# Steps of the first attention moved between the slabs of the gates' projection, and modulation pieces placed anew

## What is computed

```python
u = rms_norm(h, norm_g[i])
z = u @ w_in[i]                       # queries, keys, latents and three gates g_a, g_b, g_c (2048 columns)
o_a = mla_mixer(...)                  # 6 heads
o_b = dsa_mixer(...)                  # 5 heads, each query sees its 64 best keys of an index score
o_c = diff_mixer(...)                 # 5 heads, the difference of two softmaxes, then a norm over the head
mixed = concat([o_a * silu(g_a), o_b * silu(g_b), o_c * silu(g_c)])
h = h + mixed @ w_o[i]
h = h + (p[i] @ w_ple[i]) * sigmoid(h @ w_pg[i])
```

## Time and profile before

| | |
|---|---|
| three runs | 3386.38, 3389.06 (median), 3389.70 us |
| profiled execution | 3384.65 us, span 3383.0 us |
| TensorE busy | 3164.3 us (94%) |
| VectorE busy | 2399.3 us (71%) |
| ScalarE busy | 1366.1 us (40%) |
| granted TensorE clock, mean | 0.957 of 2.4 GHz |
| HBM read | 700.26 MB, 208 GB/s |

### The profile page before, as it was taken

One profiled execution on the slowest core, in us unless ns is written; L12 is line 12 of the kernel. 1 busy time (PEld: TensorE's weight loads), 2 busy tenths in 40 slices (PEclk: granted clock), 3 DMA queues, 4 the chain that ended last, 5 costly groups with the idle time before them and its releaser, 6 DMA issues.

```text
span 3383.0 us, 58771 instructions
## 1 busy us (share of the span) xinstructions
PE 3164.3 (94%) x24402; PEld 2997.7 (89%) x24402; DVE 2399.3 (71%) x3266; ACT 1366.1 (40%) x1459; POOL 273.1 (8%) x530
## 2 busy tenths in 40 slices
PE   5999888989998889999999999999889999899998
PEld 5999658989997569999999999998679999799998
DVE  6876768987777678875777477666767977476464
ACT  4333344444334353444334334533654333434332
POOL 0000000000000000000010010000000232010000
PEclk9999869999999779999999999999999999899999
DMA  5776404766777018766677676476025765386553
GB/s 206 271 286 242 175 19 176 275 225 243 267 269 264 25 62 306 264 229 216 257 274 249 215 273 247 176 284 248 1 101 218 259 201 200 104 294 225 208 211 130
DMA packets 130932, 710.16 MB, mean 210 GB/s; under 512 B 16392, under 2 KB 16544, under 8 KB 71584
## 3 DMA queue, kind: packets, MB, share of 16 engines
q1 hardware_dynamic: 67392, 484.47, 40.1%
q0 software_dynamic: 61264, 214.93, 17.5%
q10 hardware_dynamic: 2064, 7.70, 0.6%
HBM read 700.26 MB, written 2.10 MB: 208 GB/s over the span
## 4 chain that ended last, share of the span: by engine, by line
PE 79%; DVE 10%; ACT 5%; issue 3%; DMA 3%; ACTq 0%; DVEq 0%; POOLq 0%
PE bank L510 23%; PE bank L506 21%; PE bank L507 21%; DMA aslab<-w_ada_dram 3%; ACT whi L1014 2%; DVE wlo L1523 2%; PE bank L603 2%; PE bank L835 1%; PE bank L814 1%; DVE aslab L1548 1%; DVE sc L1642 1%; PE bank L557 1%; PE bank L922 1%; PE bank L880 1%; ACT xs L1431 1%
## 5 line engine op out<-in xcount | busy, mean ns | idle before, releaser
L506 PE MATMUL bank<-uhi,whi 128*128 128x256 f32 x6720 | 1660.9, 287 | 70.7 <-issue 47.6
L507 PE MATMUL bank<-ulo,whi 128*128 128x256 f32 x6720 | 1649.1, 285 | 0.0
L1523 DVE TENSOR_TENSOR wlo<-raw,whi 128x2048 fp32r<-128x2048 f32 (+1 forms) x464 | 1053.4, 2272 | 686.6 <-ACT whi L1014 686.1
L1014 ACT CAST whi<-raw 128x2048 fp32r<-128x2048 f32 (+1 forms) x464 | 875.6, 1889 | 1596.1 <-PE bank L510 1537.5
L506 PEld LDWEIGHTS bank<-uhi,whi 128*128 128x128 f32 x6720 | 1303.6, 194 | 79.3 <-issue 69.6
L507 PEld LDWEIGHTS bank<-ulo,whi 128*128 128x128 f32 x6720 | 1303.6, 194 | 1.1
L510 PE MATMUL bank<-uhi,wlo 128*128 128x256 f32 x6720 | 882.6, 284 | 10.7 <-DVE wlo L1523 10.5
L510 PEld LDWEIGHTS bank<-uhi,wlo 128*128 128x128 f32 x6720 | 840.7, 192 | 12.7 <-DVE wlo L1523 12.7
L450 POOL DMA_DIRECT2D aslab<-w_ada_dram x384 | 202.8, 528 | 2855.0 <-DVE mod L1548 1542.0
L1548 DVE CUSTOM_DVE_ANT_0 aslab<-aslab,sil,cols 128x1024 f32<-128x1024 f32 x192 | 245.1, 1280 | 46.2 <-DMA aslab<-w_ada_dram 46.2
L1548 DVE CUSTOM_DVE_ANT_0 aslab<-aslab,sil,part 128x1024 f32<-128x1024 f32 x192 | 244.6, 1279 | 23.0 <-DMA aslab<-w_ada_dram 22.9
(11 more groups left out here) (265 smaller groups left out, 2493.6 us busy)
## 6 DMA issues: line engine op xcount, KB each, us to landing
aslab<-w_ada_dram POOLq DMA_DIRECT2D x384, 512.0 KB, 5.0
raw<-w_win_dram SPq DMA_DIRECT2D x96, 1024.0 KB, 4.8
raw<-w_wfi_dram SPq DMA_DIRECT2D x96, 1024.0 KB, 5.1
raw<-w_wfo_dram SPq DMA_DIRECT2D x48, 1024.0 KB, 4.8
raw<-w_wci_dram SPq DMA_DIRECT2D x48, 1024.0 KB, 4.9
raw<-w_wo_dram SPq DMA_DIRECT2D x32, 1024.0 KB, 4.9
raw<-w_wpg_dram SPq DMA_DIRECT2D x32, 1024.0 KB, 5.7
raw<-w_wqz_dram SPq DMA_DIRECT2D x32, 1024.0 KB, 4.8
```

The source lines that it names most:

```text
L506: nc.tensor.matmul(o, w_, xhi_, start=start, stop=False, skip_group_check=True)
L507: nc.tensor.matmul(o, w_, xlo_, start=False, stop=False, skip_group_check=True)
L1014: nc.scalar.copy(whi[:, s % 2, 0:n], raw[:, s, 0:n]).then_inc(s_hi, 1)
L1523: v.tensor_tensor(wlo[:, s, 0:n], raw[:, s, 0:n], whi[:, s % 2, 0:n].bitcast(F32), ALU.subtract).then_inc(s_lo, 1)
```

## The change

The input projection's gate columns, which were the first 4 of its 12 groups, become a run `ga` of their own behind `up`; `in` keeps 8 groups. The 24 steps of the first attention stand between the passes of the 16 slabs of `ga`: `UNIT_AT` gives 24 of the 32 points (a point lies between the high and the low pass of a slab, and one behind the slab) a step, from point 3 to point 30. Scores now use one PSUM bank and transposes one, since the slabs take four. ScalarE applies the gates' Silu as it drains each group of `ga` (before, in one instruction of 4096 columns in `up`). The sums and roots of the norm over heads c are split in three, their sums stand at points 28 and 30, and two quarters of `uhi`/`ulo` for run `o` are filled before the reciprocals. Some tiles move: the attention's operands leave `uhi`, which `ga` needs. Modulation pieces: `in` has 28 and 25 for 40 and 40, `v` 4 for 8, `fci` 28 for 40, `fxi` 42 for 40, `kvx` 4 for 0, `qz` 40 for 34, the second attention (`attn2`) 28 for 0, `ao` 19 for 17, `ci` 14 for 11, `co` 20 for 18. The total stays 384. The Silus of the condition vectors move with them.

```diff
-        run(f"in{l}", "T", "win", 12 * l, 12, ada=40)
-        run(f"v{l}", "N", "wv", 3 * l, 3, ada=8)
+        run(f"in{l}", "T", "win", 12 * l, 8, ada=(28, 25)[l])
+        run(f"v{l}", "N", "wv", 3 * l, 3, ada=4)
         run(f"up{l}", "S", "wup", l, 1, 6)
+        run(f"ga{l}", "T", "win", 12 * l + 8, 4)
...
-            run("kvx", "K", "wkv", 0, 1)
-            run("qz", "T", "wqz", 0, 8, ada=34)
-            run("ao", "T", "wao", 0, 4, ada=17)
-            run("ci", "T", "wci", 0, 12, ada=11)
-            run("co", "T", "wco", 0, 4, ada=18)
-        run(which + "i", "T", "wfi", 8 * j, 8, ada=32 if which == "f3" else 40)
+            run("kvx", "K", "wkv", 0, 1, ada=4)
+            run("qz", "T", "wqz", 0, 8, ada=40)
+            run("attn2", "A", None, 0, 0, ada=28)
+            run("ao", "T", "wao", 0, 4, ada=19)
+            run("ci", "T", "wci", 0, 12, ada=14)
+            run("co", "T", "wco", 0, 4, ada=20)
+        run(which + "i", "T", "wfi", 8 * j, 8, ada={"fc": 28, "fx": 42, "f3": 32}[which])
...
     def upto(p):
         if r["name"] == "in0":
-            return 32 * min(max(p - 4, 0), 31) // 31 + min(max(p - 39, 0), 8)
+            return min(max(p - 3, 0), 28)
         if r["name"] == "in1":
-            return r["ada"] * max(0, p - 4) // 44
+            return 16 * min(max(p - 3, 0), 13) // 13 + min(max(p - 22, 0), 9)
         if r["name"] == "ci":
             return min(p, r["ada"])
         if r["name"] in ("pg1", "fco", "fxo"):
             return r["ada"] * min(p, 13) // 13
-        if r["name"] in ("fci", "fxi"):
-            return min(p, 16) + 24 * max(0, p - 16) // 16
+        if r["name"] == "fci":
+            return min(p, 3) + 25 * max(0, p - 8) // 24
+        if r["name"] == "fxi":
+            return 18 * min(p, 16) // 16 + 24 * max(0, p - 16) // 16
+        if r["name"] == "f3i":
+            return min(p, 16) + max(0, p - 16)
+        if r["name"] == "attn2":
+            return r["ada"] * p // NP2
...
+UNIT_AT = {3 + 29 * t // (N1 + 3): t for t in range(N1 + 3)}
+TOP_AT = {13 * i // (TOPK // 8): i for i in range(TOPK // 8 + 1)}
...
+                def unit_step(t):
+                    if t < N1:
+                        u = N1 * l + t
+                        if t:
+                            pe.wait_ge(s_sd, u)
+                        scores(t, bank[5]).then_inc(s_s, 1)
+                    if 2 <= t < N1 + 2 and HAS_T1[t - 2]:
+                        i = t - 2
+                        tn = TN[N1 * l + i]
+                        pe.wait_ge(s_pr, N1 * l + i + 1)
+                        if tn > 1:
+                            pe.wait_ge(s_tc, tn - 1)
+                        for c in range(3):
+                            last = nc.tensor.transpose(bank[6][:, P * c:P * (c + 1)],
+                                                       scs[:, i % 3, P * c:P * (c + 1)], ident)
+                        last.then_inc(s_t, 1)
+                    if t >= 3 and HAS_T1[t - 3]:
+                        pe.wait_ge(s_tc, TN[N1 * l + t - 3])
+                        values(t - 3, pts[:, TN[N1 * l + t - 3] % 2, :]).then_inc(s_o, 1)
...
+                def point(n):
+                    t = UNIT_AT.get(n)
+                    if t is None:
+                        return
+                    unit_step(t)
+                    if t == N1:
+                        pe.wait_ge(s_osq, l + 1)
+                        pe.wait_ge(s_sd, N1 * (l + 1))
+                        subln_sum(0, bank[5])
+                    if t == N1 + 2:
+                        subln_sum(1, bank[6])
+                        pe.wait_ge(s_of, NT1 * (l + 1) - 1)
+                        subln_sum(2, bank[7])
+
                 pe.wait_ge(s_ir, 8 * l + 8)
-                softmax_units(N1 * l, N1, scores, transposes, values)
-
-                pe.wait_ge(s_osq, l + 1)
-                for c in range(3):
-                    n = 512 if c < 2 else 256
-                    last = nc.tensor.matmul(bank[5 + c][:, 0:n], ones[:, :], sq[:, 512 * c:512 * c + n],
-                                            start=True, stop=True)
-                last.then_inc(s_oss, 1)
+                r = RUN[f"ga{l}"]
+                for g in range(4):
+                    group(r, g, (r["e0"] + g) % 2, slab_t, None, lambda s, g=g: point(2 * (4 * g + s) + 1),
+                          lambda s, g=g: point(2 * (4 * g + s)))
...
+                def drain_ga(g):
+                    act.wait_ge(s_s, N1 * l + (6 if g else 4))
+                    summed(ga, g)
+                    for half in range(2):
+                        at = 1024 * g + 512 * half
+                        last = nc.scalar.activation(zz_t[:, at:at + 512],
+                                                    bank[2 * ((ga["e0"] + g) % 2) + half][:, :], ACT.Silu)
+                    last.then_inc(s_drain, 2)
+
+                ga, r = RUN[f"ga{l}"], RUN[f"ple{l}"]
+                for q in range(16):
+                    if q < 14:
+                        split(ga, (q + 2) // 4, (q + 2) % 4)
+                    else:
+                        split(r, 0, q - 14)
+                    if q == 14:
+                        act.wait_ge(s_p, 16 * (l + 1))
+                        nc.scalar.copy(uhi[:, 8:10, :], praw[:, :, :]).then_inc(s_uh, 4)
+                    if q % 4 == 3:
+                        drain_ga(q // 4)
+                    point(2 * q + 1)
+                    point(2 * q + 2)
+                act.wait_ge(s_aw, 2 * l + 2)
                 act.wait_ge(s_of, NT1 * (l + 1))
-                nc.scalar.activation(sq[:, 0:5 * T], zz_t[:, T * Z_CQ:T * (Z_CQ + 5)], ACT.Square)\
-                    .then_inc(s_osq, 1)
-
-                r = RUN[f"ple{l}"]
-                presplit(f"ple{l}")
-                act.wait_ge(s_p, 16 * (l + 1))
-                nc.scalar.copy(uhi[:, 0:2, :], praw[:, :, :]).then_inc(s_uh, 4)
-                act.wait_ge(s_oss, l + 1)
+                fill_quarter(f"m{l}", zz_t, 0)
                 for c in range(3):
-                    n = 512 if c < 2 else 256
-                    last = nc.scalar.activation(sc[:, 512 * c:512 * c + n], bank[5 + c][:, 0:n], ACT.Sqrt,
-                                                bias=EPSB, scale=1.0 / P)
-                last.then_inc(s_ort, 1)
+                    subln_root(c, bank[5 + c])
+                fill_quarter(f"m{l}", zz_t, 1)
...
+                def unit_step(t):
+                    units = []
+                    if t < N1:
+                        units.append(maxes(t, N1 * l + t))
+                    if 1 <= t <= N1:
+                        units.append(scales(t - 1, N1 * l + t - 1))
+                    while units:
+                        units = [u for u in units if next(u, None) is not None]
+                    if t in TOP_AT:
+                        top_round(TOP_AT[t])
+                    if t in (14, 15):
+                        gate_first(t - 14)
+                    if t >= 3:
+                        outs(t - 3, TN[N1 * l + t - 3])
+
+                def point(n):
+                    t = UNIT_AT.get(n)
+                    if t is not None:
+                        unit_step(t)
+
+                ga, r = RUN[f"ga{l}"], RUN[f"ple{l}"]
+                for q in range(16):
+                    point(2 * q + 1)
+                    if q < 14:
+                        split(ga, (q + 2) // 4, (q + 2) % 4)
+                    else:
+                        split(r, 0, q - 14)
+                    point(2 * q + 2)
+                fill_u(f"p{l}", praw[:, :, :].rearrange("p k n -> p (k n)"), 1, 512, 4, 2048)
+                fill_quarter(f"m{l}", zz_t, 0)
+                dve.wait_ge(s_ort, 3 * l + 1)
+                ort = zz_t[:, T * Z_ORT:T * (Z_ORT + 5)]
+                link(v.reciprocal(ort[:, 0:512], ort[:, 0:512]))
                 split(r, 0, 2)
-                link(v.reciprocal(sc[:, 640:1280], sc[:, 640:1280]))
+                fill_quarter(f"m{l}", zz_t, 1)
+                dve.wait_ge(s_ort, 3 * l + 3)
+                link(v.reciprocal(ort[:, 512:1280], ort[:, 512:1280]))
                 split(r, 0, 3)
                 oc = zz_t[:, T * Z_CQ:T * (Z_CQ + 5)]
                 link(v.scalar_tensor_tensor(out=oc, in0=oc, scalar=sm[:, SM_SUBG + l:SM_SUBG + l + 1],
-                                            in1=sc[:, 0:5 * T], op0=ALU.mult, op1=ALU.mult))
+                                            in1=ort, op0=ALU.mult, op1=ALU.mult))
                 gc = zz_t[:, T * 11:T * 16]
+                dve.wait_ge(s_drain, 2 * (ga["e0"] + 4))
                 v.tensor_tensor(gc, gc, oc, ALU.mult).then_inc(s_mix, 1)
                 presplit(f"o{l}")
-                fill_u(f"m{l}", zz_t)
+                for c in (2, 3):
+                    fill_quarter(f"m{l}", zz_t, c)
...
+                if t < NP2:
+                    ada(RUN["attn2"], t)
...
```

More of the change, by code:

```diff
@@ L422, in _ @@
             for r in RUNS:
+                if not r["n"]:
+                    continue
```

(2 more changed lines are left out.)

178 lines of the change are left out of this document (81 added, 97 removed).

## The result

The changed kernel takes 3367.18 us (median of 4 runs, 3364.07 to 3369.66) beside 3387.72 us for the kernel before on the same chip: a ratio of 0.9939, 95% interval 0.9922 to 0.9956. It is 20.5 us faster; the forecast's sum had 35.4, to 3354 us. The sign and the mechanism were right, and the time lies inside the stated range of 3341 to 3369; the gain was forecast too large by some 15 us. One execution of experiment 1 took 10,834 us at a granted clock of 0.34 and is left out of all medians here.

A forecast was written before the change was run, and what follows sets the result against it. TensorE, 79% of the chain, was taken as the bound, with time won where it idles or runs slowly. 49.3 + 2.6 - 2 - 12 - 1.5 - 1 = 35.4 us gave a 3354 us median, range 3341 to 3369 (0.62).

The forecast's parts named there:

- The attention: First attention moved among the gates' slabs: 163.4 us a layer in place of 187.0 and 189.1, 49.3 us won together.
- Waits inside the steps: Attention steps in `ga`: only ScalarE's drains come close, 6.8 us against 6.8; 1 us a layer taken.
- The tail: From the last slab of `ga` to `o`: 24.8 us, where it was 28.4 from the squares on.
- Small terms: Fewer pieces in `v` win 2.6 us for both layers; presplitting `ga` ahead of the index sums costs 2.
- The second attention: Its 28 modulation pieces make a step with a piece 3.9 us on VectorE: 12 us lost, bounds 8 and 20.
- rival 2: Second attention loses the clock: all 32 steps at 1.2 GHz cost 80 us, 3434 us; half cost 40; chance 0.07.
- the 1 us for `fci`: Run `fci`: fewer pieces, but of two instructions, and a condition's Silu in ScalarE's way: 1 us lost.
- The 0 for "`qz`, `kvx`, `fxi`, `ao`, `co`": Those runs' changed piece counts cost 0 (0 to 3) us, VectorE at some two thirds with a slab of lead.
- `ci` and the rest: Three more pieces in `ci`, where VectorE is the bound: 1.5 us lost, between 0 and 4.
- The chain showed through: Rival: interleaved steps hold TensorE, 1.3 us each, 3416 us, or 0.4 each, 3373; chance 0.05 full, 0.13 at a third.
- the steps ran at full speed: Opposes a rival: attention steps take 62 us in place of 41, 42 us of gain gone, 3396 us; chance 0.05.
- More was not won: Rival: no waits, the tail at 22 us, pieces at 8, small terms 0: some 3338 us or less; chance 0.08.

The follow-up runs named there:

- experiment 1: The changed kernel run once more, unaltered, for a second profile: 3366.97 us, ratio 0.9933 to the kernel before.
- Experiment 6: Changed kernel with ScalarE draining the gates' groups by Copy in place of Silu, so no table switches there: 3365.31 us, ratio 0.9929.
- the cut kernel: The kernel before, with VectorE's instruction of every modulation piece cut from 1024 to 8 columns, transfers and waits kept: 3353.33 us, ratio 0.9895.
- the second profile: The kernel before run once more, unaltered: 3389.25 us, ratio 1.000.
- the cut kernels: The kernel before and the changed kernel, each with the pieces' VectorE instructions cut from 1024 to 8 columns: 3353.33 and 3321.34 us.
- (4): Changed kernel with only the second condition's instruction of the 35 pieces in `fci` and `fco` cut to 8 columns: 3362.11 us, ratio 0.9920.
- (8): Changed kernel with the 25 later pieces of `fci` spread over positions 6 to 28 of 32 in place of 8 to 31: 3366.57 us, ratio 0.9931.
- the second profiles: The unaltered kernel before and the unaltered changed kernel, each profiled again: 3389.25 and 3366.97 us.

## Why the prediction was right in kind and too high

**The attention: right, 38 to 43 us for 49.** The clock is 0.99 through `ga`, 16 slabs and 24 steps took 139.6 us (135 to 140 forecast), TensorE never waits for VectorE's low halves there. The layer's 163.4 us came out at 166.6. Two terms were mis-sized:

- *Waits inside the steps*, "I take 1 us": one wait of 1.74 us. The forecast had seen 6.8 us against 6.8 at the drains and counted on the tie. ScalarE's copy is ready 7.1 us behind the slab's end (463.66 to 470.73), and TensorE asks for it after 5.5 us already. Experiment 6 shows that the wait goes with the table loads. The rule that the forecast had weighed is that of the Trainium skill's "ScalarE: Activation LUTs" ("What ACT_TABLE_LOAD costs"); by the estimate from it the close drain would have cost 3 us more a layer. The trace does not agree: the load starts 0.02 us behind the instruction ahead of it, the next instruction starts at once behind its 1.28 us (465.68, 466.98), and the whole wait is 1.74 us.
- *The tail*, 24.8 for 27.0. Up to the last slab of `ple` the forecast's chain holds within 0.4 us. That slab was put at 2.9 us and took 5.45: TensorE had stood 4.15 us, and the slab ran wholly at 1.2 GHz. The sum reckoned with full clock there, though it named a low clock behind sparse use at the start of `ga`.

The figures of before vary too. In block 1 both uncut profiles have 189.1 and 189.0 us, and the 38 comes from the cut kernel, whose 184.7 block 0 shows too, in the second profile.

**Small terms.** The wait of 1.32 us in `v` is gone as forecast. In the cut kernels, which don't have that wait, the stretch ahead of `ga` is 1.6 and 1.9 us longer than before, so what was placed there costs some 1.7 us a layer, not 1. A wait fits it: TensorE stands 1.7 to 1.9 us in the index scores for an instruction of ScalarE (`pt`, line 1276), which stands behind the presplit of `ga` there. It does so in each profile of the changed placement and has no such wait at that place before. No run took the presplit away. In the full kernels the pieces' waits hide this: 1.4 us lost to 2.0 us won.

**The second attention: right mechanism, 12 forecast, 8.8 measured; with its pieces cut it gets back 8.1.** VectorE is full and pairs of steps with pieces come every 2407.59 - 2400.18 = 7.41 us in the timeline above, 3.71 a step for 3.9. The forecast added durations; in the timeline the instruction behind a piece of 1.28 us starts after 1.20 (2395.24, 2396.44). The clock, rival 2, stayed up: 1.00 from 2380 to 2460 us.

**The step that failed** is the 1 us for `fci`: "fewer pieces, but of the kind in two instructions". What they cost shows in the run behind it, `fco`, which the forecast had nothing for: 7.5 and 7.7 us in the two pairs of profiles, of the 13.0 lost from `o` of block 1 to the second attention. None of the 13 is there without the pieces' VectorE work. Two experiments give most of it back: `fco` falls from 108.4 to 102.9 us when the second instructions are cut (4) and to 102.0 when the same instructions only stand earlier (8). So it is less the doubled price than its place, ahead of the gate that `fco` starts on. The 0 for "`qz`, `kvx`, `fxi`, `ao`, `co`" failed too, in smaller pieces: the keys and queries lost 1.6 and 2.2 us, `co` 1.9 and 3.6. The rest of the 13, in `o` and `pg`, can't be told from chance.

The sum of TensorE's waits of 0.2 us and more in that stretch went from 29.1 to 41.3 us, those for the low half from 7.8 to 15.4. What the forecast left out is that VectorE's share of two thirds is a mean. A piece waits for its transfer with all of VectorE's queue behind it, and the next low half, or a gate, is the first thing in that queue. Such waits are often paid again in clock, in part: behind waits of 4.82, 2.04 and 1.33 us the pass up to the next instruction took 3.58, 2.45 and 2.02 us for 1.92. But behind the 3.21 us in `fco` the whole slab took 5.83 us at clock 1.00.

**`ci` and the rest: 1.5 forecast, 6.6 measured** (9.1 by the second profiles, nothing in the cut kernels); `ci` itself has 4.1 and 6.1 of it. A part has a name: TensorE waits 2.75 us for the shifted copies of `gp`, which GpSimd issues only behind the transfers of all `ci`'s pieces. Counted from the first matmul of `ao`, it issues the first at 2665.44 - 2498.74 = 166.7 us before and at 2659.20 - 2476.98 = 182.2 us after, right behind a piece (2658.07). A wait of 2.5 to 4.0 us stands there in every profile of the changed placement whose pieces in `ci` are uncut, and in neither of the kernel before.
The forecast weighed what the pieces cost on VectorE's queue and did not look at the one that issues their transfers. That it is these three pieces' place in the queue was not tried by itself.

**Rivals.** The chain showed through at one step of 24, with 1.74 us, the second attention kept its clock, and the steps ran at full speed as the earlier trace rows had it; none of the three holds at a strength that decides. More was not won.

**What stays open.** The profiled executions of the kernel before lie 3 to 6 us below the medians of their own batches (3384.65 against 3387.72, 3383.21 against 3389.25), those of the changed one 2 to 8 above (3369.66 against 3367.18, 3375.20 against 3366.97), so the profile's ledger has a difference of 15.2 us and the timing 20.5 to 22.1. In the cut kernels both agree within 3. It seems to be in the pieces' waits, which differ most from profile to profile, but no run shows why.

## What to carry over

Work set between the passes of a full engine costs its own time at the full clock and little more, but each later instruction of the slower engines in that stretch must be placed too: 5.5 us of a layer were won by moving the roots ahead of the last slabs and 0.7 us of VectorE work ahead of 5 us of reciprocals. "VectorE is two thirds busy" doesn't price a moved instruction: ask what it waits for (a transfer with two buffers), what stands right behind it in its queue, and who waits for that; and look at the queue that issues its transfer. A work item that doubles in price costs most where it stands ahead of something that others wait for, and moving it a few slabs can be enough. To price a background job, cut its instructions in both kernels and leave its transfers and waits: two runs separated 32 us of gain from 10 us of loss. An edit that wins in the changed kernel measures what the change lost only if the kernel before did not have that cost.

## What the runs showed of the hardware

- A stall of TensorE can cost more than its length: after 4.82 us of waiting sixteen matmuls took 3.79 us, at 1.2 GHz, where they take 1.92 at 2.4; after 4.15 us the 24 matmuls of `ple`'s last slab took 5.45 us, at 1.2 GHz. After 3.21 us in `fco` the clock was still 1.00.
- A 512 KB transfer with a median of 4.9 us from issue to landing took 14.9 us in `o` of block 1 while 3.6 MB that another queue had issued were under way, and one at the same place in the kernel before took 13.9 us. Meanwhile the transfer engines were busy 0.97 and moved 374 GB/s (the row 1243:1258 above).
- VectorE's reciprocal costs by columns: 3.35 us for 512, 2.54 for 384, 4.95 for 768, so some 6.5 ns a column, where a subtraction of 1024 columns takes 1.22 us.
- Cutting an instruction from 1024 to 8 columns took it from 1280 to 222 ns.
